# Latent attention: the diagonals of inverse softmax sums built by ScalarE instead of VectorE

## The reference, cut to what matters

```python
def attend(q_b):
    s = jnp.einsum('bqhd,bkhd->bhqk', q_b, k).astype(jnp.float32) * scale
    p = jax.nn.softmax(s, axis=-1).astype(v.dtype)
    return jnp.einsum('bhqk,bkhd->bqhd', p, v)
```

## Time and profile before

| | |
|---|---|
| median of 3 runs | 2967.96 us (2966.45 to 2968.25) |
| profiled execution | 2968.85 us, its span 2967.0 us |
| TensorE busy | 2815.5 us, 95% of the span |
| VectorE busy | 1970.1 us, 66% |
| ScalarE busy | 1415.8 us, 48% |
| mean granted clock of TensorE | 0.979 of full speed |
| attention stage of latent attention | from 1434.88 to 1474.12 us of the span |

### The profile page before, as it was taken

One profiled execution on the slowest core, in us unless ns is written; L12 is line 12 of the kernel. 1 busy time (PEld: TensorE's weight loads), 2 busy tenths in 40 slices (PEclk: granted clock), 3 DMA queues, 4 the chain that ended last, 5 costly groups with the idle time before them and its releaser, 6 DMA issues.

```text
span 2967.0 us, 46933 instructions
## 1 busy us (share of the span) xinstructions
PE 2815.5 (95%) x19805; PEld 2624.9 (88%) x19805; DVE 1970.1 (66%) x2558; ACT 1415.8 (48%) x1896; POOL 100.0 (3%) x148
## 2 busy tenths in 40 slices
PE   6999989999998999999999999998999799997997
PEld 6999979999986999998899999997999589895997
DVE  5667866565667656566665665687656677746776
ACT  4445544444455444445544444565444445444443
POOL 0000000000012000001100000000000100000000
PEclk9999999999999999999999999999999899998999
DMA  7654436676551665653356566443564455543562
GB/s 223 191 165 150 125 97 209 185 208 187 161 157 57 215 189 179 186 158 94 99 184 184 162 205 185 146 128 107 186 187 154 149 170 174 182 157 94 178 197 85
DMA packets 404725, 478.35 MB, mean 161 GB/s; under 512 B 16554, under 2 KB 331652, under 8 KB 404516
## 3 DMA queue, kind: packets, MB, share of 16 engines
q1 hardware_dynamic: 400944, 467.33, 50.7%
q0 software_dynamic: 1776, 6.77, 0.8%
q10 hardware_dynamic: 1796, 1.26, 0.1%
HBM read 474.25 MB, written 1.05 MB: 160 GB/s over the span
## 4 chain that ended last, share of the span: by engine, by line
PE 87%; DVE 7%; ACT 3%; issue 2%; ACTq 0%; POOL 0%; DVEq 0%
PE Wk L639 18%; PE Wk L641 18%; PE Wk L640 17%; PE Y L639 9%; PE Y L640 9%; PE Y L641 9%; DVE w_lo L1840 1%; PE Y L897 1%; DVE work L2081 1%; PE Y L744 1%; ACT w_hi L1309 1%; PE Wk L987 1%; PE Wk L897 0%; DVE stat L1920 0%; DVE junk L2175 0%
## 5 line engine op out<-in xcount | busy, mean ns | idle before, releaser
L1840 DVE TENSOR_TENSOR w_lo<-ring,w_hi 128x1024 fp32r<-128x1024 f32 (+2 forms) x910 | 1071.2, 1201 | 638.7 <-ACT w_hi L1309 592.2
L639 PE MATMUL Wk<-xT_hi,w_hi 128*128 128x256 f32 x4320 | 1232.9, 285 | 24.6 <-DVE xT_lo L1881 17.9
L641 PE MATMUL Wk<-xT_hi,w_lo 128*128 128x256 f32 x4320 | 1225.3, 284 | 0.0
L640 PE MATMUL Wk<-xT_lo,w_hi 128*128 128x256 f32 x4320 | 1225.2, 284 | 0.0
L1309 ACT ACTIVATE w_hi<-ring 128x1024 fp32r<-128x1024 f32 (+1 forms) x894 | 906.8, 1039 | 634.5 <-PE Wk L641 432.6
L639 PEld LDWEIGHTS Wk<-xT_hi,w_hi 128*128 128x128 f32 x4320 | 831.8, 193 | 32.3 <-issue 15.0
L640 PEld LDWEIGHTS Wk<-xT_lo,w_hi 128*128 128x128 f32 x4320 | 831.8, 193 | 4.8 <-issue 1.0
L641 PEld LDWEIGHTS Wk<-xT_hi,w_lo 128*128 128x128 f32 x4320 | 831.5, 192 | 0.0
L639 PE MATMUL Y<-w_hi,hid_hi 128*128 128x512 f32 x936 | 369.2, 394 | 6.4 <-DVE hid_lo L1935 4.4
L640 PE MATMUL Y<-w_lo,hid_hi 128*128 128x512 f32 x936 | 366.8, 392 | 0.0
L641 PE MATMUL Y<-w_hi,hid_lo 128*128 128x512 f32 x936 | 365.5, 390 | 0.0
(11 more groups left out here) (291 smaller groups left out, 2700.9 us busy)
## 6 DMA issues: line engine op xcount, KB each, us to landing
ring<-in_ffn_w_gu SPq DMA_DIRECT2D x352, 512.0 KB, 4.4
ring<-in_ffn_w_down SPq DMA_DIRECT2D x224, 512.0 KB, 4.4
ring<-in_ffn_w_up SPq DMA_DIRECT2D x96, 512.0 KB, 6.0
ring<-in_hg_w_in SPq DMA_DIRECT2D x80, 512.0 KB, 3.6
ring<-in_na_w_in SPq DMA_DIRECT2D x24, 512.0 KB, 4.3
ring<-in_hg_w_out SPq DMA_DIRECT2D x16, 512.0 KB, 3.6
ring<-in_lru_w_in SPq DMA_DIRECT2D x16, 512.0 KB, 4.1
ring<-in_kv_w SPq DMA_DIRECT2D x16, 512.0 KB, 4.8
```

Of the source, the lines that this page charges most:

```text
L639: pe.matmul(o, l_hi, r_hi, start=first, stop=False)
L640: pe.matmul(o, l_hi, r_lo, start=False, stop=False)
L641: return pe.matmul(o, l_lo, r_hi, start=False, stop=last)
L1840: ins = dve.tensor_tensor(l, r, h.bitcast(F32), ALU.subtract)
```

## The change

VectorE keeps the reciprocal in latent attention and releases a new semaphore, `s_inv`, with it. The two 128x128 products of a head are done by ScalarE: a copy of the identity with the column of inverse sums as scale. ScalarE does them for head 0 ahead of the loop, for head 2g-1 behind the exponentials of head 2g, and for head 2g behind the exponentials of head 2g+1. The wait for `s_turned` that guards the slot moves with them. Neighbourhood attention keeps the products on VectorE.

```diff
--- before.py
+++ after.py
@@ -245,6 +245,7 @@
         kn_sq, kn_saved, kn_ms, kn_mean, kn_rs, k_fin, mv_saved = (
             sem("kn_sq"), sem("kn_saved"), sem("kn_ms"), sem("kn_mean"), sem("kn_rs"), sem("k_fin"), sem("mv_saved"))
         q_sq, q_fin, q_ms, q_mean, q_root = sem("q_sq"), sem("q_fin"), sem("q_ms"), sem("q_mean"), sem("q_root")
+        s_inv = sem("s_inv")
         o_high, s_high, l_high = sem("o_high"), sem("s_high"), sem("l_high")
         kd_ready = sem("kd_ready")
         conv_raw = sem("conv_raw")
@@ -1550,9 +1551,18 @@
                             .then_inc(s_exp, 1)
                 return exps
 
-            def softmax_attention(s, exps, at_pT):
+            def softmax_attention(s, exps, at_pT, diagonals=False):
 
                 h0, pairs = heads_before(s), NA_H // 2
+
+                def inverse_diagonal(h):
+
+                    act.wait_ge(s_inv, h + 1)
+                    if h >= 2:
+                        act.wait_ge(s_turned, h0 + h - 1)
+                    for tt in range(TT):
+                        act.activation(inv_diag[:, h % 2, tt, :], ident, ACT.Copy, scale=a_stat(3, h)[:, tt:tt + 1])\
+                            .then_inc(s_prob, 1)
 
                 def turned(h):
 
@@ -1562,13 +1572,19 @@
                     act.activation(at_pT[:, h % 4, :, :].rearrange("p a b -> p (a b)"), bank(2 + h % 2),
                                    ACT.Copy).then_inc(s_turned_sb, 1)
 
+                if diagonals:
+                    inverse_diagonal(0)
                 for g in range(1, pairs + 1):
                     if g < pairs:
                         exps(2 * g)
+                    if diagonals:
+                        inverse_diagonal(2 * g - 1)
                     turned(2 * g - 2)
                     turned(2 * g - 1)
                     if g < pairs:
                         exps(2 * g + 1)
+                        if diagonals:
+                            inverse_diagonal(2 * g)
 
             def save_v(o, b, tile, n=1):
                 act.wait_ge(unit_done, units_to(tile))
@@ -1677,7 +1693,7 @@
                         key_roots(2 + i)
                     ahead(22 + 2 * i, s)
                 splits(t0 + 16)
-                softmax_attention(s, exps, ml_pT)
+                softmax_attention(s, exps, ml_pT, diagonals=True)
 
             def lru(s):
                 t0 = base[s]
@@ -2160,7 +2176,7 @@
                 normed(HG_PAIRS - 1)
                 split_pair(HG_PAIRS - 1)
 
-            def softmax_attention(s, scores, split=1):
+            def softmax_attention(s, scores, split=1, diagonals=True):
 
                 h0, g0 = heads_before(s), saves_before(s)
 
@@ -2168,6 +2184,9 @@
 
                     dve.wait_ge(s_exp, 2 * (h0 + h + 1))
                     r = a_stat(3, h)
+                    if not diagonals:
+                        dve.reciprocal(r, a_stat(2, h)).then_inc(s_inv, 1)
+                        return
                     step(dve.reciprocal(r, a_stat(2, h)))
                     if h >= 2:
                         dve.wait_ge(s_turned, h0 + h - 1)
@@ -2376,7 +2395,7 @@
                 query_means(7)
 
                 splits(t0 + 16)
-                softmax_attention(s, scores)
+                softmax_attention(s, scores, diagonals=False)
 
             def lru(s):
                 step(dve.memset(lr_x[:, :, 0:3], 0.0))
```

## The result

| | before | changed |
|---|---|---|
| median of 19 runs | 2968.14 us | 2971.21 us |
| lowest to highest | 2965.98 to 2969.41 | 2970.49 to 2976.23 |
| profiled execution, its span | 2968.85, 2967.0 | 2975.94, 2974.1 |

The ratio of the means (2972.50 to 2967.79) is 1.0016, with a 95% interval of 1.0009 to 1.0022; that of the medians is 1.0010. So it is slower, by less than the 0.2% that was set as the bound of "no change". The forecast was 2973.2 us (a ratio of 1.0018) with a range of 2970.0 to 2976.5, and the most likely case was "within 0.2%, on the slow side".

What follows compares the result with a forecast made beforehand. The prediction took TensorE to bound the kernel, with VectorE off the path. Stalls of 3.3 us (rounds 2 to 7), 1.23 (round 1) and 0.68 (round 8) sum to 5.2, on 2967.96 giving 2973.2 us, range 2970.0 to 2976.5.

Steps and rivals of the forecast that it cites:

- within 0.2%, on the slow side: Whole kernel: a difference too small for its runs to tell apart, below about 5.9 us; chance of within 0.2% 0.64.
- The bound: Latent attention's rounds: TensorE alone is the path, so removing VectorE's 7.7 us of products gains 0.
- The price of a diagonal: One 128x128 product on ScalarE takes 0.40 us; a pair occupies 0.62 and is done after 0.71.
- Rounds 2 to 7: Odd head's diagonal comes late behind the next even exponentials: 0.55 us a round (0.44 wait, 0.11 restart), 3.3 in six.
- The cover of the even diagonal: Even head's diagonals cost nothing, but thinly: ScalarE is free at S + 2.41, just when the next exponentials may start.
- Round 8: Last round: diagonals of head 14 stand behind those of head 15, so T(14) starts 0.68 us later.
- Round 1: First round: diagonals of head 1 wait behind head 2's exponentials, so the next S comes 1.23 us later.
- the forecast case: Whole kernel: the summed stalls come through, giving 2973.2 us, own range 2971.9 to 2974.8; chance 0.66.
- The clock rival: A new wait in round 1 or 8 trips a clock fall costing 1.6 us: 2974.8, two 2976.4; chance 0.14.
- a difference outside the stage: Sign of being wrong: time changes outside 1434.88 to 1474.12, a stage that should last about 5.2 us longer.
- Faster: Latent attention: VectorE held TensorE up, so relieving it gives at most 2.3 us, 2965.7; chance 0.04.
- the wait is hidden: Even exponentials come sooner, odd diagonals are on time; only rounds 1 and 8 pay, 1.9 us, 2969.9; chance 0.08.

Runs made afterwards that it cites:

- experiment 1: Changed kernel with the odd head's diagonals moved behind the odd exponentials, both heads' together; 2969.19 us against 2967.56 before the change, ratio 1.0005.
- experiment 3: Changed kernel with only odd heads' diagonals on ScalarE, even heads' back on VectorE; 2972.65 us against 2967.56 before the change, ratio 1.0018.
- Experiment 5: Changed kernel with ScalarE doing the two products of every even head twice; 2976.91 us, one run.
- Experiment 4: Kernel before the change with 20 additional 128x128 matmuls behind latent attention that nobody waits for; 2973.00 us against 2967.56, ratio 1.0016.
- experiment 6: Kernel before the change with neighbourhood attention's diagonals on ScalarE, latent attention's kept on VectorE; 2964.39 us against 2968.84, ratio 0.9986.

## Why the prediction was right

*The bound.* Right: TensorE was the path, VectorE wasn't. Taking its products away gave nothing (the maximum at S + 1.50).

*The price of a diagonal.* 0.396 us measured, 0.40 forecast; the pair occupies 0.58 (1444.18 to 1444.76) and is done after 0.68, against 0.62 and 0.71. Adding the cost of the column, read off two PSUM rows, to a plain copy from SBUF gives 0.409, 3% too much. The 0.293 us of the Trainium skill ("VectorE: DVE Perf Modes", "The TRN2 errata") is 0.10 below what one takes in the trace, but it is what one occupies: 0.29 from start to start. (The sum by that price is 3.5 us, 8 x 0.21 below 5.2, and not 3.4.)

*Rounds 2 to 7.* 5.25 a round measured, 5.27 forecast. From the second S to the last-but-one V it is 32.35 us (1440.66 to 1473.01) against 29.20 before (1440.15 to 1469.35): 3.15 more, 3.3 forecast. The experiments show that it is this step: it vanishes with the place (1) and stays with half the load (3).

*The cover of the even diagonal.* Right in kind, and near in size: ScalarE had 0.06 us to spare (1442.44 + 0.58 = 1443.02, the exponentials at 1443.08). Experiment 5 shows what is behind it.

*Round 8.* 0.65 measured, 0.68 forecast.

*Round 1* is the term that was mis-sized: 1.23 forecast, 0.72 measured (from the first S to the second 1434.67 to 1440.66, 5.99 us, against 1434.88 to 1440.15, 5.27), and 0.57 in experiment 3. From T(0) to the next S the changed kernel takes 3.14 us (1437.52 to 1440.66), 3.17 was forecast, 1.94 before: so the wait itself was right. But TensorE comes out of a half clock just here. Before, the scores of round 1 had nearly all of it: they lasted 3.54 us at a mean granted clock of 0.53, and the turn 2.10:

```profile
1434.88:1438.21 3.33, 3.33 (x10) 2.64 (x10) 2.75 (x7) 0.07 (x1) 1.06 (x2) 0.53 0.50 160
```

In the changed kernel the scores took 3.05, at 0.63, and the slow stretch reached into T(0), which took 1.68 instead of 1.16:

```profile
1437.52:1439.67 2.15, 1.68 (x10) 1.49 (x8) 1.23 (x6) 1.84 (x7) 0.00 (x0) 0.70 0.87 270
```

The slowness in T(0) cost nothing, since T(1) had to wait anyway. A wait hides what is slow ahead of it; the sum counted both. Where nothing waits it makes no difference how the slow stretch is shared out: in experiment 1 scores and turn took 2.88 and 2.74 and the round 5.25, as before.

*Total.* 4.50 in the stage against 5.2. The median came to +3.07 and the mean of the 19 runs to +4.7 (2972.5 against 2967.8). The forecast for the middle was 2 us above the median: 0.7 is the stage, 0.5 of it round 1, and the rest is how the half clock was granted elsewhere. The median of 2971.21 lies in the whole range of 2970.0 to 2976.5, but 0.7 us below the 2971.9 to 2974.8 that the forecast case was given for itself. That the number held is in part luck.

*The clock rival* named the wrong place: no new wait tripped a fall in the stage (1.00 in all six rounds), but half clock was granted for longer 600 us later, at a price of 2.9 us in the profiled execution. This is one of the signs that the prediction gave for being wrong, a difference outside the stage, and it came true: the stage does not account for all. Nothing in the profile of before told that. The forecast had no case for it, only a range that was wide enough. Experiment 4 shows such steps with a mere delay; what decides them isn't shown.

*The other rivals.* Faster, and "the wait is hidden", fell with the first timeline. The rule of the Trainium skill ("Perfetto Trace Analysis", "Optimizing Scalar/DVE Operations"), that moving work to Scalar may make sense where the vector engine is saturated, fits on both sides: with VectorE at 20.75 of 28.51 us the move gave nothing, and in neighbourhood attention, where it was busy for 41.4 of 45.1 us, it shortened the stage by 9.7 with the right order and by 3.5 with the other.

## What to carry to other kernels

When work moves to an engine with time to spare, its place in that engine's queue decides: here the same 32 instructions cost 4.5 us or 0.7, by standing behind an exponential that depends on TensorE's newest result or ahead of it. Draw one round as a loop of "who starts how long after S", and price the move by the loop that gets longer. Then look for the stage in which the relieved engine really is waited for: there the same move, with the better place in the queue, took 9.7 us off the stage. And compare small differences at equal granted clock, or by the distance between two instructions around the stage, since a change can go along with other stretches of half clock far behind it, as a mere delay did in experiment 4.

## What the runs showed of the hardware

- A ScalarE copy of 128x128 float32 from SBUF with a column as scale took 386 to 404 ns; two neighbours start 0.29 us apart.
- Two VectorE products of the same shape took 0.48 us together by themselves, and 1.38 while GpSimd worked on tensors, in the same stage of the same execution; GpSimd's own took no longer for it (685 and 688 ns).
- A head of the turn that starts behind a wait takes 0.1 us longer to the next group than the second head in flow (0.99 against 0.89, which is 2.05 - 1.16).
- With a delay of 4.4 us and no new wait the runs lay at 2970.6 to 2975.3 us instead of 2966.0 to 2968.9, ten of eleven in steps that go with the mean granted clock. With 0.66 us (experiment 1) they lay at 2966.4 to 2972.3.
- After waits of TensorE of 2.08 us the clock fell in neighbourhood attention before (the scores behind took 2.08 and 1.79 us instead of 1.13); after one of 2.12 in experiment 6 it did not (1.14).
